# Attention values on the stationary side of the matmul, two heads side by side, in a two-layer decoder trunk

## The reference

```python
logits = jnp.einsum('bqhd,bqkhd->bhqk', qa, ks) * scale + bias    # keys outside the mask are -inf
p = jax.nn.softmax(logits, axis=-1)
o_a = jnp.einsum('bhqk,bqkhd->bqhd', p, vs).reshape(B, S, 512) * jax.nn.silu(ga)
x = x + jnp.concatenate([o_a, o_b], axis=-1) @ w_out_even
```

## Time and profile before

| what | value |
|---|---|
| median of 3 runs | 526.25 us (526.12 to 527.27) |
| the profiled execution: its own time | 525.81 us |
| its span | 523.8 us |
| TensorE busy | 510.3 us of the span |
| VectorE, ScalarE, GpSimd busy | 358.1, 243.8, 291.7 us |
| mean granted TensorE clock | 0.993 of full speed |

### The profile page before, as it was taken

How to read it: one execution, slowest core, us unless ns; L and a number is a source line. 1 busy time by engine, 2 the same in 40 slices (tenths; PEclk the granted TensorE clock), 3 DMA queues, 4 the chain that set the end, 5 groups by cost and what they waited for, 6 DMA issues and landing times.

```text
span 523.8 us, 7735 instructions
## 1 busy us (share of the span) xinstructions
PE 510.3 (97%) x2855; PEld 410.4 (78%) x2855; DVE 358.1 (68%) x746; ACT 243.8 (47%) x403; POOL 291.7 (56%) x180
## 2 busy tenths in 40 slices
PE   7999999999999999999999999997999999999994
PEld 7866888788888888888888889885777677787883
DVE  3795599669958446566461064999889978669824
ACT  6734744233220434734541445366666654167413
POOL 5470755735734175655324316599999997351701
PEclk9999999999999999999999999998999999999998
DMA  8443363322222002200354302506665552502004
GB/s 267 126 141 121 121 196 126 85 79 81 81 80 82 1 0 82 82 0 1 133 190 135 106 0 81 160 17 162 159 164 162 163 150 86 192 1 80 1 0 160
DMA packets 47762, 53.13 MB, mean 101 GB/s; under 512 B 5480, under 2 KB 33155, under 8 KB 47726
## 3 DMA queue, kind: packets, MB, share of 16 engines
q1 hardware_dynamic: 47726, 52.65, 33.1%
HBM read 44.03 MB, written 2.12 MB: 88 GB/s over the span
## 4 chain that ended last, share of the span: by engine, by line
PE 77%; DVE 15%; ACT 3%; issue 2%; SPq 2%; DMA 0%; POOL 0%; POOLq 0%; ACTq 0%; DVEq 0%
PE bank L1583 29%; PE bank L1563 25%; DVE bank L1366 4%; PE bank L1781 3%; PE bank L1708 3%; DVE r_va L1114 2%; PE bank L1758 2%; DVE top L1112 2%; PE bank L1859 2%; PE bank L1872 2%; PE bank L1770 2%; SPq L509 2%; DVE r_ob L1098 1%; PE bank L1880 1%; PE bank L1599 1%
## 5 line engine op out<-in xcount | busy, mean ns | idle before, releaser
L567 POOL TENSOR_TENSOR w_lo<-w_raw,w_hi 128x2048 fp32r<-128x2048 f32 (+1 forms) x31 | 140.3, 4527 | 101.9 <-ACT w_hi L714 100.9
L1563 PE MATMUL bank<-hT_hi,w_hi 128*128 128x512 f32 (+1 forms) x280 | 111.8, 399 | 0.0
L1563 PE MATMUL bank<-hT_lo,w_hi 128*128 128x512 f32 (+1 forms) x280 | 111.4, 398 | 0.0
L1563 PE MATMUL bank<-hT_hi,w_lo 128*128 128x512 f32 (+1 forms) x280 | 110.7, 395 | 0.0
L1583 PE MATMUL bank<-w_hi,hT_hi 128*128 128x512 f32 x252 | 102.0, 405 | 0.1
L1583 PE MATMUL bank<-w_hi,hT_lo 128*128 128x512 f32 x252 | 98.4, 391 | 0.0
L1583 PE MATMUL bank<-w_lo,hT_hi 128*128 128x512 f32 x252 | 98.3, 390 | 0.0
L714 ACT ACTIVATE w_hi<-w_raw 128x2048 fp32r<-128x2048 f32 (+1 forms) x35 | 65.7, 1879 | 40.1 <-PE bank L1583 35.3
L1366 DVE SCALAR_TENSOR_TENSOR bank<-r_va,pvec,bank 128x512 f32<-128x512 f32 x98 | 71.0, 752 | 7.0 <-PE bank L1872 5.4
L647 POOL TENSOR_TENSOR r_g<-r_g 128x512 f32<-128x512 f32 x48 | 62.1, 1294 | 10.3 <-ACT r_g L907 4.6
L1563 PEld LDWEIGHTS bank<-hT_lo,w_hi 128*128 128x128 f32 (+1 forms) x280 | 52.7, 188 | 18.0 <-issue 7.4
(11 more groups left out here) (234 smaller groups left out, 767.3 us busy)
## 6 DMA issues: line engine op xcount, KB each, us to landing
w_raw<-in_w_in_even_dram SPq DMA_DIRECT2D x14, 1024.0 KB, 5.2
w_raw<-in_w_in_odd_dram SPq DMA_DIRECT2D x16, 512.0 KB, 4.6
w_raw<-in_w_out_even_dram SPq DMA_DIRECT2D x4, 1024.0 KB, 7.6
w_raw<-in_w_in_odd_dram SPq DMA_DIRECT2D x4, 1024.0 KB, 5.7
w_raw<-in_w_out_odd_dram SPq DMA_DIRECT2D x4, 1024.0 KB, 5.0
r_ka<-r_qkb SPq DMA_DIRECT2D x32, 64.5 KB, 2.0
r_x<-in_x_dram SPq DMA_DIRECT2D x4, 512.0 KB, 6.0
r_x<-bias_rows SPq DMA_DIRECT2D x4, 512.0 KB, 6.0
```

The costliest lines, as they stand in the source:

```text
L567: nc.gpsimd.tensor_tensor(v(w_lo[j % 3]), v(w_raw[j % 2]), v(w_hi[j % 3]).bitcast(F32), ALU.subtract).then_inc(lo_ready, 1)
L1563: ins = nc.tensor.matmul(proj_bank(g)[0:m, :], w[:, k, P * i:P * i + m], h[:, k, :], start=(n == 0), stop=(n == 3 * KC - 1))
```

## The change

In TensorE's product the two sides change places: 64 columns of values are stationary and 128 columns of transposed probabilities move, the output is 64 (head columns) by 128 (queries). Head 2c goes to partitions 0 to 63 and head 2c + 1 to partitions 64 to 127 of the same 128 columns of bank 7. `attend(n)` runs this product for two heads at every other step only, `probT` has four buffers in place of two. The output comes out transposed, so its division by the row sums moves to the gates: VectorE scales the gates' rows by the reciprocals (`gates_by_sums`), TensorE transposes the gates, VectorE multiplies them in the bank with the transposed outputs (`gated_transposed`). In the tail, B's chunks are transposed ahead of the last product of the attention. ScalarE makes the high parts in slots 12 to 15 in halves of 1024 columns, the first behind `soft(k + 3)`, the second, which signals `hi_ready`, behind `soft(k + 5)`. GpSimd's code is not touched.

```diff
-        probT = [r_g[:, 2048 + 512 * i:2560 + 512 * i] for i in (0, 1)]
+        probT = [r_g[:, 2048 + 512 * i:2560 + 512 * i] for i in (0, 1)] + \
+            [r_att[:, 512 * i:512 * i + 512] for i in (0, 1)]
+        oaT = r_oa[:].rearrange("p (c t) -> p c t", c=4)
...
+            def half_hi(j, half):
+                if half == 0:
+                    act.wait_ge(raw_in[j % 2], raw_full[j])
+                    wait_slot_used(act, j - 3)
+                cols = slice(1024 * half, 1024 * half + 1024)
+                ins = nc.scalar.activation(w_hi[j % 3][:, cols], w_raw[j % 2][:, cols], ACT.Copy)
+                if half:
+                    ins.then_inc(hi_ready, 1)
...
-                if s_ != 2:
+                if s_ != 2 and s_ < ATT_S0:
                     split_hi(s_ + 2)
...
                         for n in (n0 + 2, n0 + 3):
                             if n < NSTEP:
                                 soft(n)
+                        if u in (0, 1):
+                            half_hi(s_ + 2, u)
...
             def empty_oa(tb):
 
-                dve.wait_ge(pv_done, AH * (tb + 1))
-                link(nc.vector.reciprocal(row_inv[:, AH * tb:AH * tb + AH], row_sum[:, AH * tb:AH * tb + AH]))
-                inv = row_inv[:, AH * tb:AH * tb + AH].unsqueeze(2).to_broadcast([P, AH, AD])
-                nc.vector.tensor_tensor(oa[:, tb, :].rearrange("p (h d) -> p h d", h=AH),
-                                        bank[7][:].rearrange("p (h d) -> p h d", h=AH), inv,
-                                        ALU.mult).then_inc(oa_emptied, 1)
+                dve.wait_ge(pv_done, AH // 2 * (tb + 1))
+                nc.vector.tensor_copy(oaT[:, :, P * tb:P * tb + P],
+                                      bank[7][:].rearrange("p (c q) -> p c q", c=4)).then_inc(oa_emptied, 1)
+            def gates_by_sums(t0, t1):
+                h0, h1 = AH * t0, AH * t1
+                dve.wait_ge(prob_ready, h1)
+                link(nc.vector.reciprocal(row_inv[:, h0:h1], row_sum[:, h0:h1]))
+                rows = gate_a[:, t0:t1, :].rearrange("p t (h d) -> p (t h) d", h=AH)
+                inv = row_inv[:, h0:h1].unsqueeze(2).to_broadcast([P, h1 - h0, AD])
+                nc.vector.tensor_tensor(rows, rows, inv, ALU.mult).then_inc(mixed_a, 1)
...
                 dve.wait_ge(probT_done, n + 1)
-                if n >= 2:
-                    dve.wait_ge(pv_done, n - 1)
-                nc.vector.tensor_copy(probT[n % 2][:, 0:w], bank[6][:, 0:w]).then_inc(probT_ready, 1)
+                if n >= 4:
+                    dve.wait_ge(pv_done, n // 2 - 1)
+                nc.vector.tensor_copy(probT[n % 4][:, 0:w], bank[6][:, 0:w]).then_inc(probT_ready, 1)
...
+            def gated_transposed(n, c):
+
+                dve.wait_ge(hT_in_bank, R_MIX + n + 1)
+                dve.wait_ge(oa_emptied, TB)
+                b = bank[mixed_bank(n)][:]
+                nc.vector.tensor_tensor(b, b, oaT[:, c, :], ALU.mult).then_inc(gated_T, 1)
...
             dve.wait_ge(gates_silu, 2)
+            gates_by_sums(0, TB - 1)
+            dve.wait_ge(act_emptied, evacs_through(FIRST[S_GA] + TB - 1, "act"))
+            gates_by_sums(TB - 1, TB)
             empty_oa(TB - 1)
+            for n in range(4):
+                mixed_low(n, B_FIRST[n])
+            for n in range(4, KC):
+                gated_transposed(n, B_FIRST[n])
+                if n > 4:
+                    mixed_low(n - 1, B_FIRST[n - 1])
+            mixed_low(KC - 1, B_FIRST[KC - 1])
...
+            def pv_two_heads(p):
+                tb, c = divmod(p, AH // 2)
+                pe.wait_ge(probT_ready, 2 * p + 2)
...
                 for i in range(tb + 1):
-                    ins = nc.tensor.matmul(bank[7][:, AD * h:AD * h + AD], probT[n % 2][:, P * i:P * i + P],
-                                           va[:, i, AD * h:AD * h + AD], start=(i == 0), stop=(i == tb))
+                    for r in range(2):
+                        h = 2 * c + r
+                        ins = nc.tensor.matmul(bank[7][AD * r:AD * r + AD, P * c:P * c + P],
+                                               va[:, i, AD * h:AD * h + AD],
+                                               probT[(2 * p + r) % 4][:, P * i:P * i + P],
+                                               start=(i == 0), stop=(i == tb), skip_group_check=True)
             def attend(n):
                 prob_transpose(n)
-                if n:
-                    pv(n - 1)
+                if n % 2 == 0 and n:
+                    pv_two_heads(n // 2 - 1)
...
             attend(NSTEP - 1)
-            pv(NSTEP - 1)
...
-            transpose_blocks(B_FIRST, ROWS_1, rows_mixed, mixed_bank)
+            for n in range(4):
+                pe.wait_ge(act_emptied, evacs_through(FIRST[S_GA] + n, "act"))
+                for t in range(TB):
+                    ins = nc.tensor.transpose(bank[mixed_bank(n)][:, P * t:P * t + P], hx(t, B_FIRST[n]), ident[:])
+                ins.then_inc(hT_in_bank, 1)
+            pv_two_heads(NSTEP // 2 - 1)
...
+            for t in range(TB):
+                gate_transposes(t, range(4, KC - 1))
+            pe.wait_ge(oa_emptied, TB)
+            for t in range(TB):
+                gate_transposes(t, (KC - 1,))
```

More of the change, by code:

```diff
@@ L344, in hybrid_trunk @@
         oa_emptied = sem("oa_emptied")
+        gated_T = sem("gated_T")
         gates_silu = sem("gates_silu")
@@ L714, in split_hi, with mixed_high @@
                 nc.scalar.activation(v(w_hi[j % 3]), v(w_raw[j % 2]), ACT.Copy).then_inc(hi_ready, 1)
[L716 to L720, removed]
+            def mixed_high(n, c):
+                if c < 4:
+                    act.wait_ge(gated_T, c + 1)
+                else:
+                    act.wait_ge(hT_in_bank, R_MIX + n + 1)
+                nc.scalar.activation(hT_hi[:, c, :], bank[mixed_bank(n)][:], ACT.Copy,
+                                     scale=1.0 if c < 4 else pb3[:, 2:3]).then_inc(hT_hi_ready, 1)
             def half_high(base, half, half_bank, scale, chunks=range(KC)):
@@ L867, in _ @@
             wait_slot_used(act, S_OE - 1)
-            hT_high(R_MIX, B_FIRST, mixed_bank, lambda c: 1.0 if c < 4 else pb3[:, 2:3])
+            for n, c in enumerate(B_FIRST):
+                mixed_high(n, c)
             def row_squares(base, n0, half, squared=lambda t: None, rows=range(TB)):
@@ L1012, in row_variance, with mixed_low @@
                                                    in1=v, op0=ALU.mult, op1=ALU.add).then_inc(var_ready, 1)
[L1014 to L1019, removed]
+            def mixed_low(n, c):
+                dve.wait_ge(hT_hi_ready, R_MIX + n + 1)
+                nc.vector.scalar_tensor_tensor(
+                    out=hT_lo[:, c, :], in0=bank[mixed_bank(n)][:], scalar=1.0 if c < 4 else pb3[:, 2:3],
+                    in1=hT_hi[:, c, :].bitcast(F32), op0=ALU.mult, op1=ALU.subtract).then_inc(hT_ready, 1)
+            def gated_transposed(n, c):
[3 more added lines that the diff above has]
+                nc.vector.tensor_tensor(b, b, oaT[:, c, :], ALU.mult).then_inc(gated_T, 1)
             def half_low(base, half, half_bank, scale, chunks=range(KC)):
@@ L1483, in _ @@
             pe.wait_ge(pool_chain, 2)
-            def transpose_blocks(order, blocks, ready, bank_of):
-                for n, t in blocks:
-                    ready(n, t)
-                    ins = nc.tensor.transpose(bank[bank_of(n)][:, P * t:P * t + P], hx(t, order[n]), ident[:])
-                    if t == TB - 1:
-                        ins.then_inc(hT_in_bank, 1)
-            LOW, HIGH = range(4), range(4, KC)
-            ROWS_1 = [(n, t) for part in (LOW, HIGH) for t in range(TB) for n in part]
             def keep_clock(n, dst):
@@ L1771, in prob_transpose @@
                 ins.then_inc(probT_done, 1)
-            def pv(n):
-                tb, h = divmod(n, AH)
-                pe.wait_ge(probT_ready, n + 1)
-                if n == 0:
+            def pv_two_heads(p):
+                tb, c = divmod(p, AH // 2)
+                pe.wait_ge(probT_ready, 2 * p + 2)
+                if p == 0:
                     pe.wait_ge(act_emptied, evacs_through(FIRST[S_VA] + 3, "act"))
-                if h == 0 and tb:
+                if c == 0 and tb:
                     pe.wait_ge(oa_emptied, tb)
                 for i in range(tb + 1):
-                    ins = nc.tensor.matmul(bank[7][:, AD * h:AD * h + AD], probT[n % 2][:, P * i:P * i + P],
-                                           va[:, i, AD * h:AD * h + AD], start=(i == 0), stop=(i == tb))
+                    for r in range(2):
[4 more added lines that the diff above has]
+                                               start=(i == 0), stop=(i == tb), skip_group_check=True)
                 ins.then_inc(pv_done, 1)
@@ L1814, in _, with gate_transposes @@
             attend(NSTEP - 1)
-            pv(NSTEP - 1)
-            pe.wait_ge(act_emptied, evacs_through(FIRST[S_OE] - 1, "act"))
```

(17 more changed lines are left out.)

8 lines of the change are left out of this document (removed).

## The result

The changed kernel takes 529.03 us (528.80 to 530.41, five executions); the kernel before, on the same chip, 526.25 (525.95 to 527.27). The ratio is 1.0051 with a 95% interval of 1.0033 to 1.0069: about half a per cent slower. The profiled execution's span is 526.9 us, against 523.8. I forecast 529.2.

A forecast was written before the change was run, and what follows sets the result against it. TensorE's order of work was taken to bound the attention stage. Stalls of 5.3 us less 1.95 (product), 0.2 (exponential) and 0.2 (tail) gave +2.95 us, about 529.2 us; range 523.8 to 530.8, forecast case 527.3 to 530.6.

The forecast's parts named there:

- The halves hold up the masks, and these hold up TensorE: Slots 12 to 15: GpSimd's quarter waits for the late half, delaying masks, VectorE's logits and copies, then TensorE; 5.3 us.
- The stalls: TensorE's waits for VectorE in slots 12, 13, 14 and 15: 1.2, 1.8, 1.9 and 0.4 us, 5.3 together.
- the signs that I had named: Expected in the changed profile, among others: L1270 or L1264 once each over 1.3 us, TensorE idle before step 10's scores.
- rival 3: VectorE's extra operations and GpSimd's second quarter do not collide at shared ports: 527.9 us; inside the forecast's 0.58 chance.
- The product: TensorE's swapped product in slots 12 to 15: 0.055 us a record plus 0.35 a block, saving 1.95 us.
- Rival 2: TensorE's shape change costs nothing: 525.7 us, no change; chance 0.17 together with stalls half as long.
- Rival 4: The product's two halves do not overlap on TensorE: 7.8 us more, 534.6; chance 0.05 together with other losses.
- Rival 1: GpSimd's late quarter does not reach TensorE, as masks still come ahead of need: 523.9 us; chance 0.20.
- What the halves give: ScalarE avoids the 1.89 us copy between slot 13's SiLU and the next exponential, which TensorE awaited: -0.2 us.
- The tail: From the end of T(31), step 31's transposes, to slot 16's first product: 5.25 us, set by VectorE, -0.2 us.
- The sum: Whole kernel: stalls 5.3 us, less 1.95, 0.2 and 0.2, gives +2.95 us, about 529.2 us, 0.55% slower.

The follow-up runs named there:

- experiments 2: The kernel before with only the high parts made in halves at the changed kernel's places, old product and tail kept: 529.69 us, ratio 1.0068.
- Experiment 6: The changed kernel with VectorE's extra operations moved to steps 14 to 17 (L1301) and 24 to 27 (L1295): 526.81 us, ratio 1.0020 to the kernel before.
- the first experiment: The changed kernel with GpSimd's late low-part quarters queued one pair of masks later (QUARTERS_BEHIND 3, not 2): 523.49 us, ratio 0.9949 to the kernel before.
- experiment 4: The new product with whole high parts, but all records of one head before those of the other: 526.57 us, ratio 1.0008 to the kernel before.
- experiment 3: The changed kernel with the high parts whole and at their old place, so new product and tail alone: 524.26 us, ratio 0.9959 to the kernel before.

## Why the prediction was right, step by step

**The halves hold up the masks, and these hold up TensorE.** Right, and shown from both sides: halves alone give +0.68%, the changed kernel with its quarters one place later -0.51%. In slot 13 I had 4.41 us from the end of T(11) to the copy of T(12); it was 4.86 (206.64 to 211.50). The half took 1.04 for 0.95. The first mask ended at about 210.44 (209.76 + 0.68) and `logits(14)` started at 210.96, 0.5 later for my 0.15; in slots 12 and 14 that signal took 0.19, and 0.17 and 0.19 in this slot in experiments 2 and 6. Why it was longer here I did not settle.

**The stalls.** Counted from TensorE's arrival (the end of its own work ahead of the wait) to its start: slot 12 1.3 us, slot 13 1.80, slot 14 1.75, slot 15 0.63, 5.5 in all; predicted 1.2, 1.8, 1.9, 0.4 and 5.3. The difference between the changed kernel and the first experiment is the independent measure: 1.0102, 5.4 us. Two of them were right in the sum only. In slot 12 the square root's wait was smaller than I had it (0.4 for 1.0), and T(5) and the scores of step 8 waited 0.24 and 0.68, for my 0.2. The 0.68 are L1290, which stands ahead of the logits for these scores. It took 0.86 us beside GpSimd's quarter, which ran from 190.91 to 192.19:

```profile
191.35 0.86 DVE L1290 TENSOR_SCALAR stat<-stat 128x16 f32<-128x16 f32 x1
```

I had it "touch little"; it took 0.17 before, and 0.86 again in experiments 2 and 6. In slot 13 the copy came 0.45 later than in my sum and the scores only 0.08 (6.73 for 6.65): L1301 ended 0.55 after the quarter in any case (212.86 and 212.31; before, 206.64 and 206.09), so its start did not matter. Two of the signs that I had named did not come: L1301 took 1.01 us and not over 1.3 in this step, since it started 0.82 us into the quarter of 1.28, and the scores of step 10 did not wait; those of step 8 did.

**The meeting at the ports (rival 3).** Its price stands on durations. L1301 took 1.01 us and L1295 1.33 in the two critical steps, and each takes 0.68 undisturbed: 1.0 us together, where rival 3 has 1.3. L1290 adds 0.7. Each stands directly ahead of logits that TensorE then waits for. Experiment 6 does not measure the meeting by itself, since it takes the whole operation out of the critical step: the waits at the scores, 0.99 and 1.21 us, are gone. No run has the operations in their place without the meeting. The Trainium skill, SBUF — State Buffer, Who interferes with whom, says that the two engines take their shared ports as an exclusive lock. L1301 fits, by the 0.55 above.

**The product.** This is the term that was mis-sized: some -2.5 us where I had -1.95. In the first experiment T(31) starts at 258.16, before it started at 260.84, 2.68 less; of these 0.07 were there ahead of the stage and 0.2 are the wait at T(18), which leaves 2.4; added up by pairs it is 2.5. The new block was right (0.57 and 1.22 us for 0.57 and 1.23). The old ones were too cheap where they are wide. Counted pair by pair between the same weight units of the two traces, the change is +0.17, -0.05 and -0.28 us in slots 12 to 14, for my +0.15, -0.05 and -0.25. In slot 15 the three pairs gave -0.51, -0.50 and -0.77, for my -0.45 each. So most of the missing half microsecond is in slot 15, and 0.3 of it in the last pair. There TensorE waited before, and I had not seen it, since no idle time is marked:

```profile
259.80 1.00 PE L1781 MATMUL bank<-r_va,r_g 128*128 128x64 f32 x8
...
260.00 0.69 DVE L1249 COPY r_g<-bank 128x512 f32<-128x512 f32 x1 [2.03 <-PE bank L1770]
```

T(31) starts at 260.84, 1.04 us behind this product of 8 records and 0.84 behind the start of the copy of T(30). In the changed kernel T(29) starts 0.83 behind the copy that it is marked as waiting for (259.56 and 260.39). A block of 16 new records, 1.03 us up to the next transposes, covers that copy.

**Rival 2, that the change of shape costs nothing,** falls by the 1.22 us of sixteen records at 0.055. **Rival 4, no overlap,** falls by the same row; experiment 4 shows that its price of 0.109 for a record that is alone in its half was right. **Rival 1, masks in time,** is not what this kernel does, but it names the condition: where they are in time (experiment 1) the time is 523.5, and I had 523.9 for it.

**What the halves give.** The 0.2 us at T(18) are gone, as predicted. What I had not seen is that with the new product and the whole split this wait is 0.83 (experiment 3): it was costed with ScalarE's old times, and the new product makes ScalarE later.

**The tail** was to give 0.2 us and gave nothing. From the end of T(31) to the first product of slot 16 are 5.36 us (264.31 to 269.67), 5.38 before. VectorE:

```profile
265.25 0.30 DVE L1266 RECIPROCAL row_inv<-row_sum 128x24 f32<-128x24 f32 x1
265.59 1.76 DVE L1269 TENSOR_TENSOR r_qkb<-r_qkb,row_inv 128x1536 f32<-128x1536 f32 x1
...
268.10 0.69 DVE L1259 COPY r_oa<-bank 128x512 f32<-128x512 f32 x1
268.70 2.72 DVE L1035 SCALAR_TENSOR_TENSOR hT_lo<-bank,pb,hT_hi 128x512 fp32r<-128x512 f32 x4
```

VectorE's own list was even 0.1 us shorter than in my sum: the first of the four low parts ends at 268.70 + 2.72/4 = 269.38, 5.07 behind T(31), for my 5.17. But from there to the first product are 0.29 us where I had 0.08. Before, this step took 0.4, which I had taken for slack of TensorE alone; what fills it I did not settle. Behind the tail the kernel moved on whole: from the first product of slot 16 to the end 257.2 us, 257.1 before. **The sum:** stalls 5.5, product -2.5, T(18) -0.2, tail 0, so +2.8 us, and the medians differ by 2.8; I had +2.95. That the total is so close is partly luck: the product gave half a microsecond more than I had, and the stalls and the tail were 0.2 us each worse.

## What to carry to other kernels

Before an operation that many wait for is split and moved behind something late, list what stands behind its consumer in that engine's in-order queue: here GpSimd's late quarter was not needed for long, but the small masks queued behind it cost 1% of the kernel, and one place in the queue gave it back. The same holds for `empty_oa` on VectorE: moving three products by one step cost 3.3 us, though joining the ten others to their neighbours saved 2.5. Together the two placements make a kernel that is 1.0% faster than before with the very operations that made it 0.5% slower.

## What the runs showed of the hardware

- Products with 64 stationary columns and 128 moving ones cost their half of the columns 0.11 us a record, as much as a full-width transpose of 128 columns. The gain is that both halves work at once: 0.055 us a record when the halves alternate. The order mattered less than I expected. With all of one half's records queued first, blocks of 4 and 8 records took no longer; in those of 12 and 16 the second half started when three records of the first were still to come, and they took 1.15 and 1.58 us in place of 0.88 and 1.09.
- Going from one partial shape (128*64) straight to another (64*128) costs 0.20 us less than passing through the full shape between them.
- Two-input VectorE operations of 512 columns that started inside a GpSimd operation ended 0.55 us after it, wherever in it they had started: L1301 at 212.86 (quarter until 212.31), L1295 at 235.88 (quarter until 235.33) and at 238.58 (masks until 238.03). Masks do this as well as quarters. The other way round GpSimd is held up: its quarter at 214.46, which started inside L1301 (213.78 to 215.06), took 1.74 us in place of 1.28.
- L1290, with one input of 16 columns, took 0.86 us in place of 0.17 and ended at 192.21, together with GpSimd's quarter (192.19).
